# A two-block transformer kernel: first slots behind two stage boundaries by token tile, the z block first in the SSD part, unread products at two other boundaries, skip additions later

## What is computed

```python
hn = rms_norm(x, norm_mix_pre[layer])
m = retention_na_mixer(hn, ...) if layer % 2 == 0 else ssd_mixer(hn, ...)
x = x + rms_norm(m, norm_mix_post[layer])
f = conv_geglu_ffn(rms_norm(x, norm_ffn_pre[layer]), ...)
x = x + rms_norm(f, norm_ffn_post[layer])
```

```python
z, xbc, dt_raw = split(hn @ w_in)              # 2048, 3072, 64 columns
xbc = silu(depthwise_conv_centered(xbc))       # 5 taps
xs, bm, cm = split(xbc)
dt = softplus(dt_raw + dt_bias); log_a = -dt * exp(a_log)
y = bidir_scan(cm, bm, xs * dt_f, xs * dt_b, log_a_f, log_a_b)
y = y + xs * d_skip                            # the skip additions
y = y * silu(z)
y = group_rms_norm(y) * norm_g;  m = y @ w_out
```

## Time and profile before

| | |
|---|---|
| median of 3 runs | 1069.64 us (1069.45 to 1074.68) |
| profiled execution | 1067.17 us, its span 1065.4 us |
| PE busy | 1001.6 us, 94% of the span |
| POOL busy | 693.5 us, 65% |
| ACT busy | 619.5 us, 58% |
| DVE busy | 487.7 us, 46% |
| mean granted clock of PE | 0.976 |

### The profile page before, as it was taken

How to read it: one execution, slowest core, us unless ns; L and a number is a source line. 1 busy time by engine, 2 the same in 40 slices (tenths; PEclk the granted TensorE clock), 3 DMA queues, 4 the chain that set the end, 5 groups by cost and what they waited for, 6 DMA issues and landing times. The chain is left out here.

```text
span 1065.4 us, 16228 instructions
## 1 busy us (share of the span) xinstructions
PE 1001.6 (94%) x6261; PEld 884.6 (83%) x6261; DVE 487.7 (46%) x980; ACT 619.5 (58%) x1127; POOL 693.5 (65%) x548
## 2 busy tenths in 40 slices
PE   5999979999999798989899899999998998999988
PEld 4898769999998797878768799999977887877777
DVE  3745344534434466585753544434353143233543
ACT  7636666555555676576756654554555478755621
POOL 3968526665775587676657566665768756865654
PEclk9999999999999899999898899999998999999989
DMA  9774415765555365643535455555555655634310
GB/s 327 237 216 141 157 42 199 250 229 194 177 184 151 106 209 148 208 144 134 199 96 175 138 183 199 171 187 197 189 167 165 160 159 178 217 120 156 95 65 40
DMA packets 131946, 178.69 MB, mean 168 GB/s; under 512 B 21457, under 2 KB 94045, under 8 KB 131677
## 3 DMA queue, kind: packets, MB, share of 16 engines
q1 hardware_dynamic: 127693, 169.95, 49.4%
q10 hardware_dynamic: 4176, 7.71, 2.2%
HBM read 176.51 MB, written 5.24 MB: 171 GB/s over the span
## 5 line engine op out<-in xcount | busy, mean ns | idle before, releaser
L505 POOL TENSOR_TENSOR wlo<-raw,whi 128x512 fp32r<-128x512 f32 x512 | 672.6, 1349 | 345.0 <-ACT whi L1110 344.8
L520 PE MATMUL PS<-Th,whi 128*128 128x256 f32 (+1 forms) x1008 | 290.8, 289 | 3.3 <-DVE Tl L1596 2.2
L521 PE MATMUL PS<-Tl,whi 128*128 128x256 f32 (+1 forms) x1008 | 287.7, 285 | 0.0
L522 PE MATMUL PS<-Th,wlo 128*128 128x256 f32 (+1 forms) x1008 | 287.5, 285 | 0.0
L1110 ACT ACTIVATE whi<-raw 128x1024 fp32r<-128x1024 f32 (+1 forms) x150 | 157.0, 1047 | 180.9 <-PE PS L522 130.2
L517 PE MATMUL PS<-whi,Th 128*128 128x512 f32 (+1 forms) x512 | 206.4, 403 | 7.6 <-DVE Tl L1596 5.0
L1651 DVE SCALAR_TENSOR_TENSOR arena<-PS,cols,arena 128x255 f32<-128x255 f32 (+1 forms) x272 | 118.6, 478 | 190.4 <-ACT arena L1209 167.5
L520 PEld LDWEIGHTS PS<-Th,whi 128*128 128x128 f32 (+1 forms) x1008 | 194.5, 193 | 10.2 <-issue 5.7
L518 PE MATMUL PS<-wlo,Th 128*128 128x512 f32 (+1 forms) x512 | 199.5, 390 | 0.0
L519 PE MATMUL PS<-whi,Tl 128*128 128x512 f32 (+1 forms) x512 | 199.4, 389 | 0.0
L521 PEld LDWEIGHTS PS<-Tl,whi 128*128 128x128 f32 (+1 forms) x1008 | 194.5, 193 | 1.6 <-issue 0.7
(11 more groups left out here) (223 smaller groups left out, 1069.4 us busy)
## 6 DMA issues: line engine op xcount, KB each, us to landing
raw<-in_ffn_w_up_dram SPq DMA_DIRECT2D x44, 1024.0 KB, 5.1
raw<-in_ffn_w_down_dram SPq DMA_DIRECT2D x22, 1024.0 KB, 4.9
raw<-in_w_in_dram SPq DMA_DIRECT2D x22, 1024.0 KB, 5.1
raw<-in_c_w_in_dram SPq DMA_DIRECT2D x16, 1024.0 KB, 6.4
raw<-in_ab_w_in_dram SPq DMA_DIRECT2D x14, 1024.0 KB, 6.2
raw<-in_c_w_out_dram SPq DMA_DIRECT2D x8, 1024.0 KB, 5.8
raw<-in_ab_w_out_dram SPq DMA_DIRECT2D x4, 1024.0 KB, 5.0
raw<-in_c_w_in_dram SPq DMA_DIRECT2D x8, 512.0 KB, 5.2
```

Of the source, the lines that this page charges most:

```text
L505: i = nc.gpsimd.tensor_tensor(wlo[n % NLO][:, c:e], raw[n % NRAW][:, c:e], whi[n % NHI][:, c:e].bitcast(F32), ALU.subtract)
L520: mm(o, wh, ah, start=first, stop=False)
L521: mm(o, wh, al, start=False, stop=False)
L522: return mm(o, wl, ah, start=False, stop=last)
```

## The change

The diff, cut to its core:

```diff
         cwin = I["c_w_in"][0]
+        tm(("z", 0), cwin, 0)
         wide(("dt", 0), cwin, 0, SI + XBC, 8, 64)
...
-            tm(("z", g), cwin, 512 * g)
+            if g:
+                tm(("z", g), cwin, 512 * g)
...
             def norm_T(l):
...
+                    if l and t == 0:
+                        warm(4 - norm_bank(l), 3)
+
+            def tile_T(l, t):
+
+                if t:
+                    pe.wait_ge(*at("T_lo", (("n", l, 0), KD - 1)))
+                for k in range(KD):
+                    if k % 4 == 0:
+                        pe.wait_ge(*at("n_hn", (l, t, k // 4)))
+                    i = tr(PS[:, norm_bank(l) + k // 2, (k % 2) * S + t * P:(k % 2) * S + (t + 1) * P],
+                           hn[:, t, k * P:(k + 1) * P], ident)
+                    if k % 2:
+                        i.then_inc(*done("turned", (("n", l, t), k)))
+
+            def first_block(name, b0, l):
+
+                tile_T(l, 0)
+                for t in range(NT):
+                    for hf in range(2):
+                        n = slot_no[(name, hf)]
+                        if t == 0:
+                            pe.wait_ge(*low(n))
+                        h, w = whi[n % NHI], wlo[n % NLO]
+                        for k in range(4):
+                            if (t, hf, k) == (0, 1, 3):
+                                tile_T(l, 1)
+                            kk = 4 * hf + k
+                            pe.wait_ge(*at("T_lo", (("n", l, t), kk)))
+                            i = three(PS[:, b0 + t, :], h[:, k * 512:(k + 1) * 512], w[:, k * 512:(k + 1) * 512],
+                                      Th[:, kk, t * P:(t + 1) * P], Tl[:, kk, t * P:(t + 1) * P], kk == 0, kk == 7, True)
+                        if t:
+                            i.then_inc(*done("w_used", n))
 
...
-            norm_T(2)
+            first_block(("z", 0), 4, 2)
 
 
             n = slot_no[("dt", 0)]
...
                     pair(6)
-                    last_turn(0)
-                    ssd_slot(g + 1, 5)
+                    ssd_slot(g + 1, 5, mid=lambda: last_turn(0))
                     last_turn(1)
...
-            for j in range(5):
+            for j in range(3):
...
-                if j == 3:
-                    pe.wait_ge(*at("la"))
+            pe.wait_ge(*at("la"))
+            for k, (m, c, dr) in enumerate((("gt", 0, 0), ("lt", 1, 1), ("le", 1, 0), ("ge", 0, 1), ("le", 0, 0), ("ge", 1, 1))):
...
             for g in range(SG):
                 ssd(g)
...
-            norm_T(4)
-            block_tm("qa", 4, ("n", 4))
+            first_block("qa", 4, 4)
             block_tm("ka", 2)
...
+                def tile_hi(t):
+                    for k in range(KD):
+                        if k % 2 == 0:
+                            act.wait_ge(*at("turned", (("n", l + 1, t), k + 1)))
+                        a = (k % 2) * S + t * P
+                        act.activation(Th[:, k, t * P:(t + 1) * P], PS[:, norm_bank(l + 1) + k // 2, a:a + P], ACT.Identity,
+                                       scale=col(gain, k)).then_inc(*done("T_hi", (("n", l + 1, t), k)))
+
...
                 root_post(1)
+                if l + 1 in (2, 4):
+                    tile_hi(0)
+                    normed(1)
+                    high(n + 2)
+                    tile_hi(1)
+                    return
                 normed(1)
                 high(n + 2)
                 T_hi(("n", l + 1), KD, 0, norm_bank(l + 1), lambda k: col(gain, k))
...
 
+            used((("z", 0), 1))
+            copy_block(("z", 0), zt[0], 4, func=ACT.Silu)
             act.wait_ge(*at("w_used", slot_no[("dt", 0)]))
...
                     lk(product(t, 1))
+                    if tiles and t:
+                        tile_lo(0, 0, 4)
                     dve.wait_ge(*at("root", ("p", l, t)))
                     lk(nc.vector.reciprocal(st[:, 14 + t:15 + t], st[:, 10 + t:11 + t]))
                     for hf in range(2):
                         xv = x[:, t, 512 * hf:512 * hf + 512]
...
+                    if tiles and t:
+                        tile_lo(0, 4)
+
+                def tile_lo(t, k0=0, k1=KD):
+                    for k in range(k0, k1):
+                        if k % 2 == 0:
+                            dve.wait_ge(*at("T_hi", (("n", l + 1, t), k + 1)))
+                        a = (k % 2) * S + t * P
+                        stt3(out=Tl[:, k, t * P:(t + 1) * P], in0=PS[:, norm_bank(l + 1) + k // 2, a:a + P], scalar=col(gain, k),
+                             in1=Th[:, k, t * P:(t + 1) * P].bitcast(F32), op0=ALU.mult, op1=ALU.subtract)\
+                            .then_inc(*done("T_lo", (("n", l + 1, t), k)))
...
-                dve.wait_ge(*at("s_yie", g))
-                for c in range(NT):
-                    i = tt(y[:, c, :], y[:, c, :], xs[g % 2][:, c, :], ALU.add)
-                lk(i)
 
...
                 masked(3)
                 if more:
                     ssd_conv(g + 1, 1)
+                dve.wait_ge(*at("s_yie", g))
+                for c in range(NT):
+                    i = tt(y[:, c, :], y[:, c, :], xs[g % 2][:, c, :], ALU.add)
+                lk(i)
                 masked(4)
                 masked(5)
```

63 lines of the change are left out of this document (36 added, 27 removed).

## The result

The changed kernel takes 1084.66 us (median of 4 runs, 1081.7 to 1087.02), the kernel before 1069.55 in runs beside it; the ratio is 1.013, 95% interval 1.0095 to 1.0165. The prediction was 1079, in a range of 1070 to 1087. A second batch gave 1082.69 and 1.0122 (1.0071 to 1.0172). The profiled execution took 1087.02 us, the one of before 1067.17, so the two traces lie 19.8 us apart where the medians lie 15.1 apart; a difference between the traces is no difference between the kernels until other runs show it too.

A forecast was written before the change was run, and what follows sets the result against it. TensorE bounds the kernel, busy 1001.6 of 1065.4 us. Terms 9.4 - 2.1 + 5.0 + 4.2 - 3.9 - 3.7 + 1.0 = +9.9 us give 1077.1 on the profiled execution, 1079.5 by the median; predicted 1079, range 1070 to 1087.

The forecast's parts named there:

- Boundary 2 and the SSD start, +9.4: Boundary 2 to ssd(0): PE waits for late low parts and loses z's cover; ssd(0) at 403.1 against 393.7, +9.4 us.
- The boundary by tile gives nothing: Boundary 2: z and dt end at 373.7 by tile, against 372.9 in the old order.
- The clock behind these waits, +5.0: Low clock behind boundary 2 and the SSD start's second wait, 2.5 us each: +5.0 us, bounds 0 and 6.8.
- dtx, -2.1: First state products: dtx ahead of the wait takes back PE's 2.12 us wait, -2.1 us.
- Boundary 4, +4.2: Boundary 4: PE waits 8.6 us for qa's second slot, ka's low parts come late; +4.2 us, bounds +2.6 and +4.6.
- Unread products, -3.9: Boundaries 1 and 3: three products fit inside the 4.1 us wait and keep the clock up; -3.9 us, bounds 0 and -4.5.
- Skip additions, -3.7 (and +1.0): SSD groups: later additions let PE start earlier, -3.7 us; clock falling in two new waits, +1.0 (bounds 0 and 3.4).
- Rival (c): Unread products don't hold the clock and the additions meet POOL: +3.9 + 4.2 on the sum, 1087 us; chance 0.13.
- Rival (b): Boundaries 2 and 4 by tile really overlap if the second slot's low parts are there by 354.2: 1062 us; chance 0.07.
- rival (d): SSD groups 1 and 2: no new waits, each gives its 3.1 us and the clock; 5 us better, 1074; chance 0.1.

The follow-up runs named there:

- e2: Changed kernel with boundary 2 and the order at the SSD start as before; median 13.0 to 15.0 us below the changed kernel's, 0.9999 of before.
- e4: Changed kernel with z still first, but boundary 2 not by tile; way from boundary 2 to ssd(0) 51.87 us, 3.6 below the changed kernel's.
- e8: e7 with dtx and the copy of the transposed B ahead of the wait, as in the change; 1060.09 us.
- e7: Kernel before with the skip additions between masked(2) and masked(3); 1062.12 us, 0.9919 of before.
- e1: Changed kernel with boundary 4 as before; median lower by 6.8 us against its first batch and 4.8 against its second.
- e5: Kernel before with the change's later skip additions alone; 0.9987 of before.
- e3: Changed kernel with ACT rounding the second weight slot right behind tile 0's root at boundaries 2 and 4; medians 7.6 to 9.6 us below the changed kernel.
- e9: e8 with unread products at boundaries 1 and 3, four behind tile 0 and one behind tile 1; 1057.69 us.
- e10: e9 with boundary 4 by tile, its second slot rounded right behind tile 0's root, and last_turn inside the slot; 1050.56 us, 0.981 of before.
- e6: Kernel before with unread products at boundaries 1 and 3, four behind tile 0 and one behind tile 1; 0.9983 of before.

## Why the prediction was right, and where it was not

The changed kernel is slower, by about the forecast's amount and for the reason given. What the prediction has too high is two gains, the unread products and the skip additions. Little luck is in the total: these two misses, 3.7 and 2.7 us, point the same way and cover the 3.7 to 5.7 us by which the medians lie above 1079; the other terms are within about 1 us together.

**Boundary 2 and the SSD start, +9.4: right.** The waits came as 6.59 (7.4 predicted), 0.89 (0.6), 2.98 (3.5) and 5.06 (5.1), and `ssd(0)` at +11.0 from the boundary's transposes, in e2 taken back whole. Of the 11.0, 1.9 is the low clock behind the boundary, which the prediction counts in its next term; without it the 9.4 measured 9.1. Most of it is the lost cover, 7.4 us by e4. The boundary by tile takes 3.6, since PE gets to `bc` 26.8 us behind tile 0's transposes, and 23.3 in the old form. "The boundary by tile gives nothing" reads as if it took nothing, and that holds only before the clock term. Counted from 349.26, as in the prediction, the old form ends z and `dt` at 372.6 (372.9 forecast), the new one at 375.0 (373.7 at full clock), and `bc` starts at 376.1. The old form's end had the low clock of its trace in it, the new one's had not. With the 2.5 us of its clock term and the wait of 0.6 the prediction has 3.9 us here, beside 3.6 measured; what I expected of e4, at most 2.5, left the clock term out.

**The clock behind these waits, +5.0: about right.** In the changed kernel's trace the low stretch at the second slot's wait goes on for 3.9 us behind it, which costs 1.9, and the one at the second wait of the start for 4.9 us, which costs 2.4: 4.3 together. With the 9.4 the forecast for this part is 14.4 us, and e2's median lies 13.0 to 15.0 below the changed kernel's. Against before the mean clock doesn't show this term (0.974 and 0.976 for 0.973), because other parts of the change take low clock away: with boundary 2 and the SSD start back, in e2, it is 0.980. Which of the other low stretches went for which reason, the traces of single executions don't tell.

**dtx, -2.1: right**, 2.0 us by the medians of e8 and e7, 2.4 by the way of group 0.

**Boundary 4, +4.2: right**, +4.4 by the traces and by e1 (4.8 to 6.8 by the medians). The prediction's own steps give 3.6 (821 for 817.4) and don't say where the other 0.6 comes from. The wait is 6.58 us, not 8.6: the low parts came 12.0 us behind tile 0's transposes (12.4 forecast), and PE was through with its first slot at 5.4 instead of 3.8. `qa` then ends 2.3 us later than before, counted from tile 0's transposes. Most of the rest is the wait of 1.72 us for the low parts of `ka`, which the prediction names but lets end before `qa` does.

**Unread products, -3.9: mis-sized.** The ways from boundary 1 to 2 and from 3 to 4 are 0.10 and 0.15 us shorter than before. The prediction expected 1.2 us of the wait to stay open and didn't count the second one, for tile 1's low parts (`Tl`). Three products leave two gaps of 1.56 and 1.42 us, and the clock falls behind them all the same. It falls for half as long, but later: before's stretch began at 157.1, inside the wait, where it costs nothing, the changed kernel's at 160.1, when PE is at work again. With four and one the gain is there, 3.2 us for both.

**Skip additions, -3.7 (and +1.0): failed.** The step is "`pair(4)` comes 2.1 us earlier in group 2, 1.1 in group 1, 0.3 in group 0". The new wait for the additions was forecast (2.0 us; 1.95 came). But it, the wait for `masked(3)` and the clock behind them together give back all that was won in groups 1 and 2, and group 0, which had waits of 1.16 and 0.39 us only, gets one of 2.29 us in e5 and of 2.66 in the changed kernel, where the additions meet POOL and take 2.42. For the edit alone that makes 0.9987 of before. The terms of the waits in groups 1 and 2 were right, and the net was taken too high.

Put together as they measured, the terms are 9.1 + 4.3 - 2.4 + 4.4 - 0.2 + 0 = +15.2 us, where the first batch's medians lie 15.1 apart. The parts outside boundary 2 and the SSD start were forecast at -4.5 us together; e2, which has them alone, shows 0.0 (-2.6 to +2.4).

Rival (c), products that don't hold the clock and additions that meet POOL, is the nearest of the four. Its 1087 is 2 to 4 us too high, mostly because it has +1.5 for the additions, which cost nothing net, and 14.4 where 13.4 came. Rival (b), a boundary by tile that overlaps, was tied to low parts that are there by 354.2. e3 has them there 5.2 us behind tile 0's transposes (354.2 is 4.9 behind), early enough that the second slot's product doesn't wait. It gains 4.5 us over the changed kernel on B2 and 2.8 on B4, not 6.8 and 8, since the same rounding makes tile 0's own split late. What rival (d) put on the masked products, 5 us, comes with the additions in the right place: 4.9 us in e7's groups 1 and 2.

## What to carry to other kernels

A block of matmuls that waits for nothing is worth what it hides: before it is moved, find the chain that runs beside it (here convolutions and SiLU, 11 us) and see what covers that chain afterwards. Work taken off a critical place should go into a hole of the same engine, and the hole is read from the waits of that engine, not of the one that is late; behind the next milestone it only moves the wait. Where a throttled clock comes and goes, compare kernels by span times mean clock and by ways between marks besides the medians, and don't put a gain down to an edit from one trace. A mean clock that stays level against the kernel before doesn't say that a new wait costs no clock, since other parts of the same change may give clock back: take the one part back alone.

## What the runs showed of the hardware

- At boundary 1 PE's full clock was held through gaps of 0.70 and 0.55 us with products between them (e9), and fell to its lower level for 3.4 us behind gaps of 1.56 and 1.42 us at the same place (the changed kernel).
- It also fell far from any change, in code that ran at full clock in before's trace (914 and 962 us in the changed kernel's). Ahead of 914 PE had gaps of 1.08 and 1.46 us; ahead of 962 its longest gap in 45 us was 0.32, and before's trace, with nearly the same gaps at both places, stays at full clock. 68 us behind boundary 4 it fell in e3 and e10, which have the boundary by tile, and in e6, which has not.
- The mean granted clock was 0.973 in before and 0.989 in e10, which has fewer waits in several places. At a span of 1067 us that is worth about 17 us, most of e10's 20, while span times clock moved by 2.
- Two additions on DVE with both inputs in SBUF took 1.28 us with POOL idle, and 1.81 (e5), 2.42 (the changed kernel, group 0), 2.77 (before) and 3.37 (e7, group 3) where POOL was at work for part of the time or all of it.
